# Gated retention output with two gate chunks first and two gate buffers; score product signals the free weight buffer in the memory heads

## What is computed

```python
gates = jax.nn.sigmoid(h[..., OFF_GATE:] + b_gate[l]).reshape(B, S, N_BRANCHES, D_MODEL)
y_ret = (jax.nn.silu(r_g) * ret.astype(x.dtype)) @ w_ret_o[l]
mix = (gates[:, :, 0] * y_sb + gates[:, :, 1] * y_ret) @ w_mix_o[l]

def memory_cross_attention(x, mem, w_q, w_kv, w_o):      # x (1024 x 1024), mem (256 x 1024)
    q = (x @ w_q).reshape(B, S, MEM_HEADS, MEM_HEAD_DIM)
    kv = (mem @ w_kv).reshape(B, MEM_LEN, 2, MEM_HEADS, MEM_HEAD_DIM)
    s = jnp.einsum('bshd,bmhd->bhsm', q, k) * (MEM_HEAD_DIM ** -0.5)
    p = jax.nn.softmax(s, axis=-1)
    o = jnp.einsum('bhsm,bmhd->bshd', p, v).reshape(B, S, D_MODEL)
```

## Time and profile before

| | us |
|---|---|
| median of 3 runs | 2115.11 (2114.38 to 2115.65) |
| the profiled execution | 2117.16 |
| its span, first to last instruction | 2115.3 |
| PE busy | 2000.3 (95%) |
| DVE, ACT, POOL busy | 998.0, 700.3, 996.7 |
| mean granted TensorE clock | 0.981 |

### The profile page before, as it was taken

How to read it: one execution, slowest core, us unless ns; L and a number is a source line. 1 busy time by engine, 2 the same in 40 slices (tenths; PEclk the granted TensorE clock), 3 DMA queues, 4 the chain that set the end, 5 groups by cost and what they waited for, 6 DMA issues and landing times.

```text
span 2115.3 us, 25838 instructions
## 1 busy us (share of the span) xinstructions
PE 2000.3 (95%) x10056; PEld 1648.6 (78%) x10056; DVE 998.0 (47%) x1098; ACT 700.3 (33%) x1075; POOL 996.7 (47%) x543
## 2 busy tenths in 40 slices
PE   7999999999999999998978998979999999999986
PEld 6888888788777787886768886858888888888866
DVE  5657567200166656235373335278545544411646
ACT  2313224001055555211152223164343334332334
POOL 4233232343254445345856443867545555544432
PEclk9999999999999999999979999989999999999998
DMA  5122121222101000311112210132221222354442
GB/s 183 31 88 69 40 79 30 69 70 69 50 21 31 21 21 25 124 42 40 51 51 79 69 60 20 50 116 74 80 90 70 83 87 89 119 201 138 127 161 101
DMA packets 54229, 159.76 MB, mean 76 GB/s; under 512 B 5632, under 2 KB 11904, under 8 KB 53120
## 3 DMA queue, kind: packets, MB, share of 16 engines
q1 hardware_dynamic: 47344, 134.47, 19.4%
q10 hardware_dynamic: 6800, 24.12, 3.0%
HBM read 134.45 MB, written 24.12 MB: 75 GB/s over the span
## 4 chain that ended last, share of the span: by engine, by line
PE 82%; DVE 8%; issue 3%; ACT 3%; POOL 2%; DMA 2%; DVEq 0%; POOLq 0%; SPq 0%; ACTq 0%
PE unit L676 13%; PE unit L682 12%; PE unit L680 12%; PE unit L1085 3%; PE unit L1087 3%; PE unit L1086 3%; PE aux L1086 3%; PE aux L1085 3%; PE aux L1087 3%; PE aux L870 2%; PE aux L876 2%; PE aux L874 2%; PE unit L1163 1%; PE unit L1164 1%; PE unit L1165 1%
## 5 line engine op out<-in xcount | busy, mean ns | idle before, releaser
L492 POOL TENSOR_TENSOR w_hi<-w_raw,one 128x1024 fp32r<-128x1024 f32 x70 | 137.3, 1961 | 490.6 <-PE unit L676 490.6
L676 PE MATMUL unit<-x_lo,w_hi 128*128 128x512 f32 x752 | 294.3, 391 | 13.1 <-POOL w_lo L506 11.6
L680 PE MATMUL unit<-x_hi,w_hi 128*128 128x512 f32 x752 | 293.5, 390 | 0.0
L682 PE MATMUL unit<-x_hi,w_lo 128*128 128x512 f32 x752 | 293.4, 390 | 0.0
L495 POOL TENSOR_TENSOR w_lo<-w_raw,w_hi 128x1024 fp32r<-128x1024 f32 x70 | 177.1, 2529 | 5.5
L676 PEld LDWEIGHTS unit<-x_lo,w_hi 128*128 128x128 f32 x752 | 141.6, 188 | 43.5 <-POOL w_lo L506 11.6
L682 PEld LDWEIGHTS unit<-x_hi,w_lo 128*128 128x128 f32 x752 | 141.5, 188 | 29.7
L680 PEld LDWEIGHTS unit<-x_hi,w_hi 128*128 128x128 f32 x752 | 141.6, 188 | 29.3
L633 POOL TENSOR_TENSOR beta<-beta,stick 128x128 f32<-128x128 f32 (+7 forms) x64 | 77.1, 1205 | 151.8 <-DVE stick L1889 151.8
L1889 DVE TENSOR_TENSOR_SCAN stick<-stick 128x128 f32<-128x128 f32 (+7 forms) x64 | 106.4, 1663 | 49.8 <-ACT stick L1308 49.8
L676 PE MATMUL unit<-a_lo,w_hi 128*128 128x512 f32 x256 | 102.6, 401 | 9.6 <-DVE a_lo L1952 9.6
(11 more groups left out here) (542 smaller groups left out, 5493.4 us busy)
## 6 DMA issues: line engine op xcount, KB each, us to landing
w_raw<-stream SPq DMA_DIRECT2D x141, 512.0 KB, 3.5
w_next<-stream SPq DMA_DIRECT2D x34, 512.0 KB, 4.0
hidden_store<-hidden SPq DMA_DIRECT2D x22, 512.0 KB, 2.7
h_raw<-hidden_store SPq DMA_DIRECT2D x44, 256.0 KB, 3.8
rope_sb<-rope ACTq DMA_DIRECT2D x8, 1024.0 KB, 6.4
w_next<-stream SPq DMA_DIRECT2D x12, 384.0 KB, 3.4
acc<-xT ACTq DMA_DIRECT2D x8, 512.0 KB, 10.3
ret_branch<-acc ACTq DMA_DIRECT2D x8, 512.0 KB, 2.6
```

The lines of the kernel that those rows point to most:

```text
L492: pool.tensor_tensor(w_hi[s][:, 0:width], w_raw[:, s, 0:width], one[:].to_broadcast([P, width]), ALU.mult).then_inc(w_hi_done, 1)
L676: x = pe.matmul(out, w_hi[s][:, wk], lo[:, k, cols], start=first, stop=False, skip_group_check=True)
L680: pe.matmul(out, w_hi[s][:, wk], hi[:, k, cols], start=False, stop=False, skip_group_check=True)
L682: last = pe.matmul(out, w_lo[s][:, wk], hi[:, k, cols], start=False, stop=(k == kts - 1), skip_group_check=True)
```

## The change

Three things are changed.

1. The order of weight chunks and of the PE's work in the gated retention output: gate 0, gate 1, then output n and gate n+2 for n = 0 to 5, then outputs 6 and 7. Outputs 0 to 6 go to unit 0, gates 1 to 7 to unit 1, and gate 0 to unit 0, output 7 to unit 1. The first two and last two chunks stand outside the loop.
2. `gate_ret` has two buffers, used in turn; ACT's and DVE's loops over n are written out. ACT takes gate n+2 before it issues the store of row n.
3. In a memory head with `more`, the signal `chunk_started` that was given by the first matmul of key chunk 1 is given by the third matmul of `scores(0)`.

```diff
-            gate_ret = sb(st, "gate_ret", [P, SEQ])
+            gate_ret = sb(st, "gate_ret", [P, 2, SEQ])
...
-            with pe.Fori(0, KT) as n:
-                u = free_unit(U_GRET, 2, n, 0)
-                project(n * 2 + CH_GRET, 0, halves(u), x_hi, x_lo).then_inc(unit_ready, 1)
-                u = free_unit(U_GRET, 2, n, 1)
-                project(n * 2 + (CH_GRET + 1), 1, halves(u), ret_hi, ret_lo, arrived=ret_split).then_inc(unit_ready, 1)
+            for k in range(2):
+                u = free_unit(U_GRET, 0, 0, k)
+                project(CH_GRET + k, k, halves(u), x_hi, x_lo).then_inc(unit_ready, 1)
+            with pe.Fori(0, KT - 2) as n:
+                u = free_unit(U_GRET + 2, 2, n, 0)
+                project(n * 2 + (CH_GRET + 2), 0, halves(u), ret_hi, ret_lo, arrived=ret_split).then_inc(unit_ready, 1)
+                u = free_unit(U_GRET + 2, 2, n, 1)
+                project(n * 2 + (CH_GRET + 3), 1, halves(u), x_hi, x_lo).then_inc(unit_ready, 1)
+            for k in range(2):
+                u = free_unit(U_GRET, 0, 0, 2 * KT - 2 + k)
+                project(CH_GRET + 2 * KT - 2 + k, k, halves(u), ret_hi, ret_lo).then_inc(unit_ready, 1)
...
-                def scores(hf):
+                def scores(hf, ends_chunk=False):
...
+                            if ends_chunk and tt == dt == 0:
+                                x.then_inc(chunk_started, 1)
...
-                scores(0)
+                scores(0, ends_chunk=more)
                 scores(1)
                 if more:
-                    mem_chunk(h + 1, 1, u, 1).then_inc(unit_ready, 1)
+                    mem_chunk(h + 1, 1, u, 1, begins=False).then_inc(unit_ready, 1)
...
+            def gate_of(n):
+                j = n > 0
+                act.wait_ge(unit_ready, U_GRET + (2 * n if j else 1))
+                if n > 1:
+                    act.wait_ge(unit_drained[0], U_GRET // 2 + n)
+                act.activation(gate_ret[:, n % 2, :], unit[:, j, :], ACT.Sigmoid, bias=par[:, 56 + n:57 + n]
+                               ).then_inc(unit_drained[j], 1)
+
+            def save_branch(n):
+                act.wait_ge(unit_drained[n == KT - 1], U_GRET // 2 + (KT if n == KT - 1 else n + 2))
+                act.dma_start(ret_branch[n], acc[:, n, :]).then_inc(acc_saved, 16)
+
+            gate_of(0)
+            gate_of(1)
+            for n in range(2, KT):
+                gate_of(n)
+                save_branch(n - 2)
+            save_branch(KT - 2)
+            save_branch(KT - 1)
...
+            for n in range(KT):
+                j = n == KT - 1
+                dve.wait_ge(unit_ready, U_GRET + (2 * KT if j else 2 * n + 3))
+                if n:
+                    dve.wait_ge(unit_drained[1], U_GRET // 2 + n)
+                else:
+                    dve.wait_ge(unit_drained[0], U_GRET // 2 + 1)
+                dve.tensor_tensor(acc[:, n, :], unit[:, j, :], gate_ret[:, n % 2, :], ALU.mult).then_inc(unit_drained[j], 1)
...
-    for n in range(KT):
-        eight += [win[BLK_GATE_RET + n], ret_o[n]]
+    gates = [win[BLK_GATE_RET + n] for n in range(KT)]
+    eight += gates[0:2]
+    for n in range(2, KT):
+        eight += [ret_o[n - 2], gates[n]]
+    eight += [ret_o[KT - 2], ret_o[KT - 1]]
```

## The result

The changed kernel takes 2104.23 us (median of 5, 2101.4 to 2105.84), the kernel before 2115.11 us (median of 5, 2114.36 to 2117.48). The ratio is 0.9949 with a 95% interval of 0.9938 to 0.9959, so 10.9 us less. The forecast was 2103.5 us, with a range from 2102.2 to 2107.0. The profiled execution has a span of 2102.4 us. The time alone can't tell the forecast (2102.6 to 2104.3) from its first rival (2104.3 to 2106.0), as single executions of the changed kernel lie from 2101.4 to 2105.84: the traces decide.

The account below looks back on a forecast made before the run. The PE holds 82% of the chain that ended last, so only removing its idle gaps gains. 6.1 us (output stage) plus 5.5 us (three memory heads) make 11.6, taking 2115.1 to 2103.5 us; range 2102.2 to 2107.0.

Parts of the forecast that it names:

- first rival: Memory heads: both DVE-POOL draws lost in one to three heads, each gaining 1.0 instead of 1.85 us; chance 0.41.
- Part A: Gated retention output: two gates first remove the PE's stall for `ret_lo` in output chunk 0, gaining 6.1 us.
- The wait list: PE's waits by releaser: 5.2 us for `ret_lo` in output chunk 0, omitting the slow first matmul behind each wait.
- Part B: Three memory heads: the early signal lets POOL split chunk 2 sooner, 1.85 us a head, 5.5 us in all.
- The draws: Half 0's third and fourth scalings against POOL's `w_hi` and `w_lo` of chunk 3: first likelier lost (3 in 4), second even.
- second rival: Memory heads: the early signal buys nothing, leaving 2109.0 us; chance 0.03.
- The clock beside the rival: Idle 2.0 us before half 0's transposes lowers the clock, costing up to 2 us a head; chance 0.08.
- fourth rival: Memory heads: the clock falls ahead of `turn_p(0)` and stays low, making the kernel slower, 2128.5 us; chance 0.02.
- the third: Output stage: gate chunk 1 doesn't cover the end of the last head, leaving about 2109.6 us; chance 0.03.

## Why the prediction was right, point by point

- **Part A, 6.1 us.** Output 0 lost 17.22 - 11.21 = 6.0 us; the prediction's 6.1 took the chain's 382.43 for a start and an output chunk of 11.27, and the two nearly cancel. POOL's last start in the stage moved from 526.53 to 520.29, by 6.2 us, and the order alone measured 6.6 us (4.2 to 8.9). Right. The slack was mis-sized: I took the low parts to end near 379.6 with one split of POOL on them, a second only as an "if", and at least 5 us of cover; the second came, they ended at 383.39, and 2.2 us were left. The hole stays closed, so the sum did not suffer. The written-out loops cost nothing: the PE was busy for all of 387 to 526.
- **The wait list.** That it has 5.2 us and not 6.0 comes for the smaller part from the slow first matmul behind each wait (0.47 to 0.50 us instead of 0.40), some 0.3 us. For the rest, the list counts from the end of the matmul ahead (0.39 us behind its start), where the next one would have started 0.23 us behind it: 0.16 us for each of the three waits, 0.5 in all.
- **Part B's path.** POOL without idle time into chunk 2, no wait ahead of it, the sign change at about 2 us (1.95), the wait for chunk 3's `w_lo` still there: each as foretold. The head period fell by 1.8 us (forecast 1.85). Measured by itself the signal gave 3.6 us (1.7 to 5.5), forecast 5.5.
- **The draws: here there was luck.** I gave the first one to POOL at 3 in 4 and had the third scaling at 1131.37 to 1131.45 against POOL at 1131.33 to 1131.39. The changed kernel is 9.39 us earlier at the split of key chunk 1 (1110.50 against 1119.89), so what was measured, 1121.98 and 1122.02, is 1131.37 and 1131.41 on that clock: one at the edge of its range, the other 0.02 us outside. DVE won in all three heads, by 0.02 to 0.04 us. By the prediction's own odds the forecast's outcome had 0.25 by this branch and 0.375 by the other (first draw lost, second won). The time was right, but by the less likely branch, and 0.2 us of delay would have given the first rival. Its price, 1.0 us a head kept instead of 1.85, was shown by the delayed scalings. Where the prediction says "the second rival below" of two lost draws, its first rival is meant.
- **The clock beside the rival.** With the delayed scalings 2.04 us of idle time were followed by a granted clock of 0.58 and 0.62 over 4 us in two of three heads and by 1.00 in one; the price was 1.5 us in the first head (2.4 less 0.9), up to 2 forecast. The prediction's total for it does not add up: three heads at up to 2 us on top of 2106.0 give up to 2112, not 2108 to 2109. In the changed kernel there was no such idle time, and the clock stood at 1.00 from chunk 2 to the value products in all three heads, so the fourth rival (clock low for 6 us or more) had nothing to start from.
- **The second rival** (the signal buys nothing) and **the third** (the end of the last head not covered) fell by the two parts measured apart.
- **What the sum does not hold.** The span fell by 12.9 us, 1.3 more than the sum. PE's windows show where a clock differed that the change has no part in, first the kernel before, then the changed one, both at the entry of the stick-breaking stage (before 575, after 568.7) and at the end of the merged output (before 960, after 952), and last the changed kernel alone, in the last memory head:

```profile
575.00:580.00 5.00, 5.00 (x17) 0.50 0.00 0
960.00:980.00 20.00, 15.65 (x58) 0.91 0.07 26
...
568.70:573.70 5.00, 5.00 (x21) 0.68 0.00 0
952.00:972.00 20.00, 15.65 (x65) 1.00 0.08 27
1258.00:1262.00 4.00, 4.00 (x23) 0.57 0.00 0
```

POOL's starts give the distances: 6.2 us gained ahead of the stick-breaking stage, 9.6 at 968, ahead of the heads; by PE's starts 15.1 behind the three heads (1257.04 against 1272.14), and by POOL's 12.4 behind the last one. So some 3 us came between the two closed holes, and 2.7 us went in the last head, behind them, both for the most part where the clock differed. A single pair of profiles can't be held against the sum to better than that.

## What to carry to other kernels

Where a stage begins with work whose input is late, look for chunks that do not need that input and put as many of them first as cover the lateness; but count the buffers that this holds open, as one gate buffer too few turned a gain of 10 into a loss of 17 us. A "buffer free" signal belongs to the first instruction behind the last reader, whatever that instruction computes. When an engine is given work earlier, list what the others do in that time: here two engines hold each other up for the whole of an instruction, and by turning who started first 0.2 us of delay cost 0.9 us a head, and 2.4 us where the clock fell as well. Moving the work to a third engine took the draw away.

## What the runs showed of the hardware

- A DVE scaling or sign change and a POOL product or difference exclude each other for a whole instruction, and the first to start has it. Ahead of POOL by 0.02 us (1170.11 against 1170.13) a scaling took 0.35 us; 0.01 us behind it took 2.04. The small sign change of 4 columns took 0.17, 0.35, 0.72, 0.82 or 1.95 us for this alone. That is the rule that the prediction names from the Trainium skill ("SBUF — State Buffer", "Who interferes with whom"), and the runs agree with it. A held instruction went through in the gap of 0.08 us before POOL's next one (1120.66); a scaling queued right behind a held one did not, and stood for the next POOL instruction too (4.93 and 4.94 us for four).
- Not only DVE's fast instructions are held, as one expectation has it. The low parts of `ret`, differences of two inputs in SBUF, took 1.21 us at the least and up to 3.42 while POOL split, and POOL's `w_lo` beside them 3.26 instead of 2.39 us. The second split cost the eight of them 3.9 us (16.97 against 13.04).
- The granted clock after equal idle times differed: 1.00, 0.62 or 0.58 behind 2.04 us in the run with the delayed scalings, and behind the first wait for `ret_lo` ahead of output 0 (2.8 us in both) it was 1.00 in the kernel before and 0.50 from 368 to 372 in the run with the signal alone. POOL's split behind the next chunk's start began at 382.81 in both, since `ret_lo` was the pace: here a fall of the clock in a stretch that waits for another engine cost nothing.
- Executions of one kernel spread by up to 10 us here (2098.62 to 2108.67), in step with their mean granted clock (0.985 to 0.981).
